# Values of the first token block projected inside the turn of the window layer's input, and their weights loaded first

## What is computed

```
def swa_sink_mixer(h, positions, w_qkv, q_norm, k_norm, sinks, w_out):
    qkv = h @ w_qkv
    q, k, v = split(qkv)                       # 16 heads of 64; 4 heads of 64 for k and for v
    q = apply_rope_2(rms_norm_2(q, q_norm), cos, sin)
    k = apply_rope_2(rms_norm_2(k, k_norm), cos, sin)
    o = banded_sink_attention(q, k, v, sinks)  # window of 128, softmax with a sink per head
    return o @ w_out

# the step before and this layer, in second_block
gate = sigmoid(rms_norm_2(x, norm_ple[0]) @ ple_w_gate[0])
x = x + gate * (p[0] @ ple_w_proj[0])
h = rms_norm_2(x, norm_mix[1])
x = x + swa_sink_mixer(h, ...)
```

## Time and profile before

| | |
|---|---|
| median of three executions | 2178.11 us |
| lowest, highest | 2172.37, 2179.90 us |
| the profiled execution | 2174.63 us, span 2172.2 us |
| granted TensorE clock, mean | 0.991 |
| busy: PE, DVE, ACT | 98%, 80%, 63% of the span |
| the stretch of the change | 1811 to 1892 us of the span |

### The profile page before, as it was taken

One profiled execution on the slowest core, in us unless ns is written; L12 is line 12 of the kernel. 1 busy time (PEld: TensorE's weight loads), 2 busy tenths in 40 slices (PEclk: granted clock), 3 DMA queues, 4 the chain that ended last, 5 costly groups with the idle time before them and its releaser, 6 DMA issues.

```text
span 2172.2 us, 30498 instructions
## 1 busy us (share of the span) xinstructions
PE 2125.9 (98%) x12288; PEld 1866.0 (86%) x12288; DVE 1744.1 (80%) x2282; ACT 1369.9 (63%) x1771; POOL 53.7 (2%) x43
## 2 busy tenths in 40 slices
PE   7999999999999999999999999989999999999999
PEld 6989998888888888888888888879899998889997
DVE  4776656769989999999999999978677778768776
ACT  3654445548888888888888888847454445454443
POOL 0001002001000000000000001000000000000000
PEclk9999999989999999999999999999999999999999
DMA  8347664539999999999999999934446545235553
GB/s 287 129 134 242 204 204 150 170 128 388 394 395 396 395 392 384 381 378 383 378 387 370 394 370 389 373 95 158 137 156 207 181 162 173 78 115 200 190 180 117
DMA packets 283556, 561.82 MB, mean 259 GB/s; under 512 B 8988, under 2 KB 114080, under 8 KB 283168
## 3 DMA queue, kind: packets, MB, share of 16 engines
q1 hardware_dynamic: 276800, 535.33, 68.9%
q0 software_dynamic: 3568, 15.74, 1.9%
q10 hardware_dynamic: 3040, 8.72, 1.1%
HBM read 552.93 MB, written 10.49 MB: 259 GB/s over the span
## 4 chain that ended last, share of the span: by engine, by line
PE 91%; DVE 5%; DMA 1%; ACT 1%; issue 1%; SPq 0%; DVEq 0%; ACTq 0%
PE psum L421 19%; PE psum L423 19%; PE psum L422 19%; PE psum L415 9%; PE psum L416 9%; PE psum L417 9%; DVE wl L404 1%; PE psum L1866 1%; DMA raw<-in_w_in 1%; PE psum L884 1%; PE psum L2676 0%; PE psum L675 0%; PE psum L2609 0%; DMA arena<-scratch 0%; PE psum L352 0%
## 5 line engine op out<-in xcount | busy, mean ns | idle before, releaser
L404 DVE TENSOR_TENSOR wl<-raw,wh 128x1024 fp32r<-128x1024 f32 x640 | 769.1, 1230 | 173.5 <-ACT wh L396 167.3
L396 ACT ACTIVATE wh<-raw 128x1024 fp32r<-128x1024 f32 x640 | 659.1, 1050 | 270.7 <-PE psum L417 129.6
L404 DVE TENSOR_TENSOR wl<-arena,wh 128x1024 fp32r<-128x1024 f32 x384 | 456.6, 1222 | 37.4 <-ACT wh L396 30.7
L415 PE MATMUL psum<-xh,wh 128*128 128x256 f32 x1600 | 459.2, 287 | 4.3 <-DVE wl L404 1.4
L396 ACT ACTIVATE wh<-arena 128x1024 fp32r<-128x1024 f32 x384 | 403.5, 1062 | 85.0 <-PE psum L423 81.3
L416 PE MATMUL psum<-xl,wh 128*128 128x256 f32 x1600 | 455.0, 284 | 0.0
L417 PE MATMUL psum<-xh,wl 128*128 128x256 f32 x1600 | 454.8, 284 | 0.0
L421 PE MATMUL psum<-wh,xh 128*128 128x512 f32 (+1 forms) x1136 | 447.5, 394 | 0.6 <-DVE wl L404 0.3
L423 PE MATMUL psum<-wh,xl 128*128 128x512 f32 (+1 forms) x1136 | 441.2, 388 | 0.0
L422 PE MATMUL psum<-wl,xh 128*128 128x512 f32 (+1 forms) x1136 | 440.8, 388 | 0.0
L415 PEld LDWEIGHTS psum<-xh,wh 128*128 128x128 f32 x1600 | 309.2, 193 | 11.3 <-DVE wl L404 2.3
(11 more groups left out here) (410 smaller groups left out, 1570.4 us busy)
## 6 DMA issues: line engine op xcount, KB each, us to landing
arena<-in_moe_g SPq DMA_DIRECT2D x72, 1024.0 KB, 9.5
arena<-in_moe_u SPq DMA_DIRECT2D x72, 1024.0 KB, 9.6
raw<-in_moe_d SPq DMA_DIRECT2D x64, 1024.0 KB, 9.8
arena<-in_moe_d SPq DMA_DIRECT2D x48, 1024.0 KB, 8.8
raw<-in_ff_up SPq DMA_DIRECT2D x48, 1024.0 KB, 5.1
raw<-in_moe_g SPq DMA_DIRECT2D x40, 1024.0 KB, 8.2
raw<-in_moe_u SPq DMA_DIRECT2D x40, 1024.0 KB, 9.9
raw<-in_ff_down SPq DMA_DIRECT2D x24, 1024.0 KB, 4.9
```

What stands on the lines that cost most here:

```text
L396: A.activation(unit(s, i)[0], raw_half(s, i), ACT.Copy).then_inc(*s.w_hi.tick(i))
L404: V.tensor_tensor(lo, raw_half(s, i), hi.bitcast(F), SUB).then_inc(*s.w_lo.tick(i))
L415: T.matmul(ps, wh, x[0][:, k, :], start=k == 0, stop=False)
```

## The change

It does four things, all at the start of the window layer.

1. The load of the values' weights "wi.v" becomes the first of the layer; those of the keys (qk2a, qk2b) and of the first queries follow. U is now the first unit of the values.
2. `values(h)` is replaced by `pe_values(t)`, which does one token block over all 1024 inputs, into one half of bank 1. `pe_values(0)` runs between the two last quarters (1, 0) and (1, 1) of the turn, `pe_values(1)` after the four pieces of the keys' projection. The units of the values are given back only by `pe_values(1)`.
3. DVE makes the low parts of the quarters (0, 0) and (0, 1) after the third PLE piece, and no longer after the fourth.
4. The second bank of the keys' projection is 5 instead of 1, ACT takes the keys' squares after unit U + 7 in one go and copies the values after unit U + 9, and DVE's units are set at other places to fit.

```
@@ all_loads
+            w.add("wi.v", cols(x, 1536, 256), (8, 256), "rows")
             for n in (2, 0):
                 w.add(f"wi.qk{n}a", cols(x, 512 * n, 256), (8, 256))
                 w.add(f"wi.qk{n}b", cols(x, 512 * n + 256, 256), (8, 256))
-            w.add("wi.v", cols(x, 1536, 256), (8, 256), "rows")
@@ pe_rows
-    def pe_rows(st, Z, banks, t):
+    def pe_rows(st, Z, banks, t, between=None):
         for b in range(2):
+            if b and between is not None:
+                between()
@@ banks
-    QK_BANKS = {2: (0, 1), 0: (2, 3), 1: (0, 4)}
+    QK_BANKS = {2: (0, 5), 0: (2, 3), 1: (0, 4)}
@@ new
+    def pe_values(t):
+        if t == 0:
+            take(1)
+            for b in range(2):
+                T.wait_ge(*dve.of(f"nm1.x0{b}"))
+        for h, u in enumerate(un["wi.v"]):
+            T.wait_ge(*main.w_lo.of(u))
+            for k in range(4):
+                x = step_b(bk(1)[:, t * 256:(t + 1) * 256], at_t(XX, 4 * h + k, t), tuple(q[:, k, :] for q in unit(main, u)),
+                           h == 0 and k == 0, h == 1 and k == 3)
+            if t:
+                x.then_inc(*pe.tick(("unit", u), "wi.v"))
+        empties(1, (act, "wi.v"))
@@ pe_window
         for c in range(1, 4):
             qk(2, c)
+        pe_values(1)
         qk(0, 0)
         rope(2)
...
         spread_keys()
-        values(0)
         rope(0)
         sums(0)
-        values(1)
         qk(1, 0)
@@ act_window
         hi_to(main, U + 8)
         squares(2, 0)
+        squares(2, 1)
         hi_to(main, U + 10)
-        squares(2, 1)
+        A.wait_ge(*dve.of("nm1.rr"))
+        for t in range(2):
+            A.activation(WV[:, t, :], bk(1)[:, t * 256:(t + 1) * 256], ACT.Copy, scale=RR[:, t:t + 1]).then_inc(*act.tick("wi.v"))
         hi_to(main, U + 12)
...
-        A.wait_ge(*pe.of("wi.v"))
-        for t in range(2):
-            A.activation(WV[:, t, :], bk(t)[:, 0:256], ACT.Copy, scale=RR[:, t:t + 1]).then_inc(*act.tick("wi.v"))
@@ dve_window
         gained(2, 0)
-        lo_to(main, U + 9)
+        lo_to(main, U + 8)
         gained(2, 1)
         cosines(2)
-        lo_to(main, U + 11)
+        lo_to(main, U + 10)
@@ tensor_program
-        pe_ple(0, lambda t: pe_rows("nm1", ar(2048, 2, 1024), NM1, t))
+        pe_ple(0, lambda t: pe_rows("nm1", ar(2048, 2, 1024), NM1, t, (lambda: pe_values(0)) if t else None))
@@ vector_program
+                for t, h in ((0, 0), (0, 1), (1, 0), (1, 1)):
+                    dve_ple(0, t, h)
+                    V.wait_ge(*dve.last())
+                    dve_gain("nm1", Z, t, h, flat(Tz))
+                    if (t, h) == (1, 0):
+                        dve_rows("nm1", NM1, 0, 0)
+                        dve_rows("nm1", NM1, 0, 1)
+                for b in range(2):
+                    dve_rows("nm1", NM1, 1, b)
                 dve_window()
```

More of the change, by code:

```diff
@@ L2579, in program @@
     WZ_BANK = [[2, 3], [1, 4]]
-    QK_BANKS, RO_BANKS, SS_BANK = {2: (0, 1), 0: (2, 3), 1: (0, 4)}, {2: (6, 7), 0: (6, 7), 1: (0, 4)}, {2: 4, 0: 4, 1: 5}
+    QK_BANKS, RO_BANKS, SS_BANK = {2: (0, 5), 0: (2, 3), 1: (0, 4)}, {2: (6, 7), 0: (6, 7), 1: (0, 4)}, {2: 4, 0: 4, 1: 5}
     def win_scales(n):
         return (SC[:, 256 + 64 * n + 16 * i:272 + 64 * n + 16 * i] for i in range(4))
+    def pe_values(t):
[11 more added lines that the diff above has]
+        empties(1, (act, "wi.v"))
     def pe_window():
@@ L2743, in act_window @@
     def act_window():
-        U = un["wi.qk2a"][0]
+        U = un["wi.v"][0]
         def squares(n, i):
@@ L2913, in dve_window @@
         dve_rows_scale("nm1", RV, RR, RW1, RW2)
+        dve.name("nm1.rr")
         V.tensor_scalar(RW, RV, 1e-6, None, MUL).then_inc(*dve.tick())
```

## The result

| | before | change |
|---|---|---|
| median, 10 executions each | 2175.14 us | 2184.30 us |
| lowest, highest | 2172.37, 2179.90 | 2180.54, 2189.80 |
| ratio to before, 95% interval | | 1.0044, 1.0035 to 1.0053 |
| span of the profiled execution | 2172.2 us | 2181.9 us |
| mean granted TensorE clock of the 10 | not listed (0.991 in the profiled one) | 0.984 to 0.988, median 0.987 |

The change is slower by 0.44%, 9.2 us by the medians and 9.7 by the two profiled spans. The forecast was +4.7 us, about half of it.

What follows compares the result with a forecast made beforehand. TensorE bounds the kernel (91% of the last-ending chain); +4.7 us at the keys, through the rest +4.7 to +4.8, on the middle execution's 2176.4 gave 2181.1 us (+0.22%), range 2174.5 to 2187.5.

Steps and rivals of the forecast that it cites:

- The keys wait for their weights: Before the keys' projection: qk(2, 0) needs U + 2, split late, so the keys start at 1824.6 instead of 1819.87, +4.7 us.
- Queries wait for U + 6: Before the queries: ACT can't split U + 6 until the values return their units; TensorE waits about 1.2 us more.
- Low halves and first half of the values free: At the turn: low halves fit DVE's 1.57 us idle time; the values fill the 2.61 us hole, last quarter 0.4 us later.
- Loads and bank 5: Load order and the keys' second bank: both free, U + 12's load with 2.6 us to spare, bank 5 already emptied.
- DVE's uncovered chain: From the last queries to the first mask: without the values' products as cover, the mask comes at 1869.5 instead of 1864.72, +4.8 us.
- TensorE alone at +2.1 us: At the first logits: if TensorE set the pace, qk(1, 0) would start at 1862.5 and end 2.1 us later than before.
- if TensorE ends last the cost is nearer 2 us: Test before the logits: if TensorE, not DVE, ends last there, the reading of the middle is wrong, cost nearer 2 us.
- The clock: At the keys: half clock behind the moved hole costs 1.4 us as before, difference 0; bounds 0 and about 3 us.
- everything behind the mask as it was: From the first mask on: the chain stays as before, so the shift goes through unchanged to the values' weighing.
- Rival A: Longer half clock at the keys, +1.6 us, and at the softmax waits, +1.5; together +7.8, 2184.2 us; chance 0.2.
- within 0.3%: Measured time of the whole kernel indistinguishable from no change, under 0.3% or 6.5 us away; chance 0.69.
- rival C: At the keys: U + 2 and U + 3 split before the tanh, first mask at 1862.7, -2.0 us, 2174.4; chance 0.05.

Runs made afterwards that it cites:

- e2: The change, with high parts of U + 2 and U + 3 and the low part of U + 2 made before the last quarter's halves: ratio to before 1.0003.
- e5: The change, with pe_values(1) moved from behind the keys' four pieces to ahead of them: ratio to before 1.0013.
- e7: The change with e2's early units, DVE's units moved as in e6, and pe_values(1) ahead of the keys as in e5: ratio to before 0.9979.
- e1: The kernel before with only DVE's low halves of the first token block made ahead of the fourth PLE piece: ratio to before 0.9996.
- e4: The change, with DVE's low parts of U + 12 to U + 15 moved behind masks and maxima, out of its chain to the first mask: ratio to before 1.0031.
- e8: The change with 12 matmuls of no use in TensorE's hole ahead of the keys: ratio to before 1.0014.
- e3: The change with 24 matmuls of no use in TensorE's hole ahead of the keys, which started the keys later: ratio to before 1.0040.
- e9: The change with four matmuls of no use in TensorE's wait for the exponentials of piece 3, ahead of its transposes: ratio to before 1.0026.
- e6: The change with the edits of e2 and e4 together, but U + 12 made ahead of the last queries' gain: ratio to before 1.0003.
- e12: The same kernel as e7, run again: ratio to before 0.9973.
- e10: e7 with e9's four matmuls of no use ahead of the transposes of piece 3: ratio to before 0.9980.

## Why the prediction was right, and where it was short

**The keys wait for their weights: right.** Forecast: 5.6 us of standstill, keys at 1824.6. Measured: 5.38 us and 1824.22, with the whole profile 0.38 us earlier. e2 shows the cause: with those two units made earlier the loss is gone.

**Queries wait for U + 6: right.** 1.2 forecast, 1.13 measured; e5 and e7 removed it by giving U back earlier.

**Low halves and first half of the values free: right.** e1; the third quarter to the values took 0.8 us, the last quarter came 0.5 us later counted from the third, for 0.4 forecast. Loads and bank 5: no wait on either shows in TensorE's or ACT's rows up to the mask.

**DVE's uncovered chain: right in the place, hidden in its weight by the clock.** DVE ended last, without a pause, and the mask came at 1870.13 for 1869.5 forecast. But I had set TensorE alone at +2.1 us, and e4 shows it only 0.8 us ahead of DVE's chain: the logits started 5.1 us later than before (53.6 us behind the third quarter against 48.6). Of the 3 us that I missed, 1.5 are the half clock in `qk(1, 0)` and 1.1 that at the keys. So my own test, "if TensorE ends last the cost is nearer 2 us", was wrong for this kernel. In e8, without half clock, the logits start 49.7 us behind the third quarter and TensorE is 2.1 us ahead, near the 2.7 that the forecast had (+2.1 against +4.8): there the chain that lost its cover is what ends last. Why the clock falls at 1864.2 stays open. The rotation and the sums now follow the spreading without the values' products between them, which is a possible cause, but e3, e7 and e8 have the same order there and no such stretch.

**The clock: the term that failed.** I put the difference at the keys at 0, because the earlier trace rows showed one stretch of 3.2 us behind 3.8 us without work. The hole of 5.4 us gave 6.8 us at 0.50 instead. By e8, keys and values cost 2.6 us more than at the full clock, against about 1.5 before: +1.1. And I left everything behind the mask as it was. There the 17 us at half clock cost the rest: 19.4 us from piece 3's transposes to the projection against 15.0 before (1880.59 to 1895.63), +4.3. The sum by the profiles is 4.7 (the start of the keys, 9.7 us behind the third quarter against 5.0) + 1.1 + 4.3 = 10.1 us at the projection, which the table has (90.9 - 80.8), less the 0.4 by which the profile was earlier: 9.7, the difference of the spans. These are two profiles, but typical ones: the change's was at 2184.2 us and 0.986 where the median of its ten is 2184.3 and 0.987, and the kernel before was at 0.991, its medians in the later sets being 0.990 and 0.991.

Rival A named this mechanism and its two places, with 1.6 and 1.5 us; they came with 1.1 and 4.3. It had 0.2. That its result, 2184.2, is what came (2184.3) is partly luck: its shift was 7.8 us, the measured one 9.2, and it started from 2176.4 where the kernel before has a median of 2175.14. Its reason for the second stretch, a wait for the exponentials that grows from 1.5 to some 4 us, was not right either: that wait is 1.95 us. In e9's profile work in this wait goes with a shorter stretch. Why the stretch is 17 us long with a wait of 1.95 us and 6.8 with one of 1.5 stays open, for e1 has 17.1 us in one of its longest executions with the wait of 1.5 us, as before.

The upper edge at 2187.5 held the result because A was inside the range; the forecast itself had the right direction and the right waits, and half the size. The most likely case, "within 0.3%", was not what happened: a cost of 4.7 us beside a threshold of 6.5 leaves no room for a term put at zero.

**What rival C described comes true once the wait is repaired.** It did not happen in the change. It said that without the wait the first mask would come 2.0 us earlier than before. In e2, which has only 0.55 us of wait, it comes 1.6 us earlier, but the half clock behind the softmax is 10.2 us against 6.8, 0.4 us are left at the projection, and the time gains nothing; e7, with the queries' wait gone and DVE's units moved too, gained 5.

How much of the 9 us is hole and how much clock has no single answer, since the hole makes the clock fall: e2 takes away 9 us by repairing the schedule alone, e8 takes away 6.5 by keeping the clock and leaving the hole. The nearest to a price of the schedule alone is what e8 has left, with the mean clock of the kernel before (both medians 0.991): 3.0 us, between 0.4 and 5.7 by its interval, beside the 4.7 of the forecast.

## What to carry to other kernels

When work is moved up into a hole, look at what it displaces from the list of things prepared in advance: here two slots of split weights were ready, and giving them to the filler made the next user late by more than the hole was long. Work that is moved ahead also stops covering whatever ran beside it, and a buffer that it holds over a longer stretch blocks the one who fills it. Put the released resource back early (here: both halves of the product ahead of the next projection), and price a longer standstill with the clock that follows, not only by its length.

## What the runs showed of the chip

Time and mean granted clock of single executions go together. Over the 35 executions of the kernel before in the second set (e5 to e8) the correlation is -0.93, and a mean clock lower by 0.001 goes with 2.1 us (the other two sets have -0.93 and 2.0 to 2.1); in the change, from 2180.5 us at 0.988 to 2189.8 at 0.984, it is -0.96. Much of what looks like scatter between runs is how long TensorE stood at its lower level. So one profile's stretches are a sample: e1 and e5 had 17 us behind the softmax in theirs, e2 and e6 10, and a price read from one profile can be wrong by several us either way. Nor does it all happen in the stretch read here: e7 and e12 are one kernel, their profiled executions took 2177.52 and 2166.77 us, and both have 10.2 us of half clock and the same way from the third quarter to the projection (76.8 and 76.7 us); the third quarter stands at 1821.92 in the one and at 1811.17 in the other.

In this kernel the lower level came behind standstills of 1.5 to 5.4 us, but not behind every one of them (2.6 us in e1 and 2.2 in e5 were followed by the full level), and also behind the spreading, rotation and sums with only a wait of 0.18 us (1864.2 to 1867.6 in the change), and the weighing matmuls, 128x64, took 3.68 us at the one level and 6.93 at the other.

The Trainium skill ("TensorE: Matmul & The Clock Gate", section "Why this matters for your kernels") says to keep TensorE continuously busy. e8 agrees: 12 matmuls of no use gained 6.5 us over the change, with intervals that do not overlap. The 4 us of e9 are not clear of the scatter, and e10 shows no gain in the medians.
